# Branch A's product as a stage of its own, with the first head's rotation beside it

## The chip, the cores and the metric

The kernel runs on one core of one Trainium2 chip. The metric is the device time of one execution in microseconds (us); lower is better. The engines named here are TensorE (PE in the profile), VectorE (DVE), ScalarE (ACT), GpSimd (POOL) and SyncE (SP). The last two issue most of the transfers of this kernel and compute almost nothing. ScalarE also issues some stores.

## The reference, cut to what matters

One inference step of a two-layer encoder over 640 tokens: 512 of a prompt and 8 streams of 16. Each layer runs two branches on the same input projection, merges them with gates, projects the result and then runs an MLP.

```python
def _token_mixer(h, shift_prev, s_rwkv, s_ret, pos, p):
    z = h @ p['w_in']
    ...
    y_a, new_rwkv = _rwkv7_branch(za_mix, s_rwkv, p)      # 16 heads of 64, recurrent
    y_b, new_ret = _retention_branch(zb, s_ret, pos)      # 4 heads, key 256, value 512
    merged = (gates[:, :, 0] * (y_a.astype(h.dtype) @ p['w_branch_a'])
              + gates[:, :, 1] * (y_b.astype(h.dtype) @ p['w_branch_b']))
    out = merged.astype(h.dtype) @ p['w_out']

def _retention_branch(zb, s0, pos):
    q, k, v, g = ...
    q, k = rope(q), rope(k) * B_KEY_DIM ** -0.5           # "rotation" below
    # per head: scores, mask with decay, values, old state, new state
    y = y * lax.rsqrt(jnp.mean(y * y, axis=-1, keepdims=True) + NORM_EPS)
    out = jax.nn.silu(g) * y
```

"Branch A's product" is `y_a @ w_branch_a`, a 640 x 1024 by 1024 x 1024 product. The kernel calls it job `ba`.

## The kernel before

Everything lies transposed: channels on the 128 partitions, the 640 tokens along the free axis. A large product is a job of tiles. One tile is 128 output channels, and it is computed as three f32r products per 128 input channels (high x high, low x high, high x low parts), each in two halves of 320 tokens. Job `ba` has 8 tiles of 8 input blocks, so a tile is 48 matmuls. Each of the four jobs `bb0` to `bb3` (a retention head's share of branch B's product) has 8 tiles of 4 input blocks.

**Order within a layer.** Input projection and eight recurrent pairs, then `fz` (the last fill job, beside the group norm of the last pair), then the four retention heads 0 to 3, then `bb3`, the merge, `out`, the MLP. Each engine has its own written-out program, and semaphores join them.

**Units beside a chain.** A head has long chains between engines, so product work is strewn into it. The PE program of a head calls `point("s0")`, `point("y1")` and so on, and each call emits a fixed number of units of a product job (`POINTS`, times `each`). A unit is two input blocks, so 12 matmuls, and a tile of `ba` is four units. Head `h` has `bb{h-1}` beside it; head 0 has `ba`, with `each` = 2. All these units write PSUM banks 0 and 1, so before tile i+1 begins, PE waits (`psum_clear`) until VectorE has taken tile i out. VectorE and ScalarE have programs with the same points:

- VectorE (`sums_of`): at the last unit of a tile it waits for the tile (`mm_done`) and for a gate tile in `ZT`, and writes `ACC[i] = psum * gate` (L2111). At the first unit of the next tile it makes the low part of the weights of two tiles ahead (`split`, L1754, released by ScalarE's high part).
- ScalarE (`high_parts_of`): at the end of each tile it makes the high part of the weights of two tiles ahead (L1274), once they have landed and the tile has been computed.
- SP loads weights into two raw slots. For `ba`, tile i (i of 2 or more), it first waits until tile i-2 has been taken out, then issues the gate load (L504) and the weight load (L505). The last two gate-like tiles made by `fz` are also stored to DRAM by SP (L499), each of them in front of a weight load that comes four tiles later in SP's order. The last of these stores therefore stands behind the loads of `ba`'s tile 2.
- POOL clears `QDP` when the last pair is through, and loads cos and sin, head 0's queries and keys (`QK`), the head's constants, the values (`VY`), and the gate of `ba`'s tile 0 (L607). Then it waits for SP's last store (`z_out`), and only then loads the gate of `ba`'s tile 1 (L607), head 0's swish gate (L594) and the first three blocks of the old retention state (L601).

**A head.** Eight groups of transpositions (values and keys, L677), copied out by ScalarE; then scores, masks and values. Eight steps through the old state (`step`, `st0` to `st7`) go through three buffers `SR`: POOL reads a block (L601), PE multiplies, VectorE updates it (L1743), ScalarE stores it (L1550), and only when the store has landed does POOL read the block three steps on. After the values come square, root, reciprocal and scaling of each token block, the transposition back, the gate, and the split into high and low parts (`lo0` to `lo4`). VectorE rotates the next head's queries and keys in four quarters of six instructions (`rope`), and a last piece of four, in the second half of the head. Head 0's rotation has no head before it. It stands in front of head 0 on VectorE:

```python
                ve.wait_ge(rw_out, 96 * PAIRS * (l + 1))
                for _ in rope(l, 0):
                    pass
                for h in range(RH):
                    retention(l, h)
```

VectorE therefore takes tile 0 of `ba` out only after the whole rotation, and PE's second group of transpositions in a head waits for the rotation.

Of the kernel before, what the change touches and what calls it, by code (L numbers as in the profile page):

```python
# [18 lines left out]
KD = D // 128  # L19
# [212 lines left out]
def build(nc, io, outs, scratch):  # L232
    START, FREED_BY, KT = number_jobs()
# [7 lines left out]
    with ExitStack() as ctx:  # L241
# [44 lines left out]
        AW, _ = cut(at, 2 * 4096)  # L286
# [45 lines left out]
        ZT, _ = cut(SCR - 2 * TOK, 2 * TOK, TOK)  # L332
# [24 lines left out]
        NSR, _ = cut(2 * KD * TOK + 3200, A_COLS)  # L357
        SHR, _ = cut(KD * TOK, A_COLS)
        MS, _ = cut(2 * KD * TOK, KD * TOK, TOK)
        G1, _ = cut(KD * TOK, KD * TOK, TOK)  # L360
# [91 lines left out]
        def units_in(name):  # L452

            n, kt = next((j[1], j[2]) for j in jobs_of_layer() if j[0] == name)
            return n, kt // 2

        def part_of(l, name, emit, each=1):

            tiles_, units = units_in(name)
            at_ = [0]  # L460

            def point(where):
                count = POINTS[where if where in POINTS else where.rstrip("0123456789")] * each
                for _ in range(min(count, tiles_ * units - at_[0])):
                    emit(at_[0] // units, at_[0] % units)
                    at_[0] += 1
            return point

        def beside_head(h):

            return f"bb{h - 1}" if h else "ba"

        def stage_value(stage, n, name):

# [9 lines left out]
        def wait_stage(eng, stage, n, name):  # L484

            eng.wait_ge(stage_sem[stage], stage_value(stage, n, name))
# [177 lines left out]
        def _(pe):  # L664
# [101 lines left out]
                return last  # L766

            def units_of(l, name, each=1):
                g0, units = START[l, name], units_in(name)[1]

                def unit(i, q):

                    g = g0 + i
                    if q == 0:
                        pe.wait_ge(lo_done, g + 1)
                        psum_clear(g)
                    for k in (2 * q, 2 * q + 1):
                        if i == 0 and name == "ba":
                            pe.wait_ge(ya_lo, PAIRS * l + max(4, k + 1))
                        for n_, (w, part) in enumerate(((WH, 0), (WH, 1), (WL, 0))):  # L780
                            for hf in range(2):
                                last = mm(ps[:, hf, 0:HALF], w[:, g % 2, k], operand_of(name, k, part)[:, HALF * hf:HALF * hf + HALF],
                                          start=(k == 0 and n_ == 0), stop=(q == units - 1 and k == 2 * q + 1 and n_ == 2))
                    if q == units - 1:
                        last.then_inc(mm_done, 1)
                return part_of(l, name, unit, each)
# [377 lines left out]
            for l in range(DEPTH):  # L1164

                pe.wait_ge(par_in, 13 * 16 * (l + 1))
                if l:
                    wait_mark(pe, "ve", l - 1, "varf")
                tr(ps[:, 0, 0:106], PR[0:106, 0:128])
                last = tr(ps[:, 0, 106:162], PR[0:56, 128:256])  # L1170
                mark(last, l, "par")
                wait_mark(pe, "ac", l, "silu")
                for k in range(KD):
                    last = tr(ps[:, 2, NSTREAM * k:NSTREAM * k + NSTREAM], CR[0:NSTREAM, 128 * k:128 * k + 128])
                mark(last, l, "ct")
                if l == 0:
                    pe.wait_ge(x_in, 32)
                    wait_mark(pe, "ac", l, "par")
                    wait_mark(pe, "ac", l, "ct")
                    for b in range(NBLK):  # L1180
                        if b == 4:
                            wait_mark(pe, "ac", l, "x0")
                        for k in range(KD):
                            last = tr(ps[:, 2 * (b % 4) + k // 4, 128 * (k % 4):128 * (k % 4) + 128], XR[:, b, 128 * k:128 * k + 128])
                        mark(last, l, f"x{b}")
                    wait_mark(pe, "ac", l, "x4")
                wait_mark(pe, "ac", l, "par")
                wait_mark(pe, "ac", l, "ct")

                for n in range(13):  # L1190
                    m = 12 * l + n
                    if n < 12:
                        pe.wait_ge(ada_in[n % 2], 16 * (6 * l + n // 2 + 1))
                        if n >= 2:
                            pe.wait_ge(ada_row, m - 1)
                        a = AW[:, 4096 * (n % 2):4096 * (n % 2) + 4096].rearrange("p (k n) -> p k n", k=8)
                        for k in range(KD):
                            last = mm(ps[0:NSTREAM, 5 + n % 2, :], CT[:, k], a[:, k], k == 0, k == KD - 1)
                        last.then_inc(ada_used, 1)
                    if n:  # L1200
                        pe.wait_ge(ada_row, m)
                        for j in range(4):
                            t = 4 * (n - 1) + j
                            last = tr(ps[:, 7, NSTREAM * t:NSTREAM * t + NSTREAM], CR[0:NSTREAM, 512 * ((n - 1) % 2) + 128 * j:512 * ((n - 1) % 2) + 128 * j + 128])
                        last.then_inc(ada_turned, 1)
                pe.wait_ge(shr_in, 16 * (l + 1))
                for t in range(A_T):
                    last = tr(ps[:, 2, 8 * t:8 * t + 8], SHR[0:DEC_B, 128 * t:128 * t + 128])
                mark(last, l, "shr")
                wait_mark(pe, "ac", l, "mod")  # L1210
                norm_sums(l, "n0", "sq0", S1)

                gemm(l, "lora", [(l, f"h0.{j}") for j in range(4)])
                gemm(l, "rkv0")
                wait_mark(pe, "ac", l, "lora")
                pe.wait_ge(lw_in, 48 * (l + 1))
                point = units_of(l, "fa")
                for _ in prepare(l, 0):
                    point("pre")
                point("end")  # L1220
                for p in range(PAIRS):
                    rwkv(l, p)
                point = units_of(l, "fz")
                for _ in group_norm(l, PAIRS - 1):
                    point("post")
                point("end")
                wait_stage(pe, "ac_ch", PAIRS * l + PAIRS - 1, "sout")
                for h in range(RH):
                    retention(l, h)
                gemm(l, f"bb{RH - 1}", [(RH * l + RH - 1, "lo4")] * 2)  # L1230
                gemm(l, "out", [(l, f"ms{j}") for j in range(4)])
                psum_clear(START[l, "up0"])
                for t in range(A_T):
                    last = tr(ps[0:NSTREAM, t // 4, 128 * (t % 4):128 * (t % 4) + 128], NSH[:, t])
                mark(last, l, "nsh")
                wait_mark(pe, "ac", l, "nsh")
                norm_sums(l, "mix", "sqm", ACC)
                wait_mark(pe, "ve", l, "varm")
                norm_sums(l, "n1", "sq1", S1)
                for f in range(8):  # L1240
                    gemm(l, f"up{f}", [(l, f"h1.{j}") for j in range(4)] if f == 0 else ())
                    gemm(l, f"down{f}")
                psum_clear(START[l, "down7"] + 8)
                norm_sums(l, "ffn", "sqf", ACC)
# [10 lines left out]
        def _(ac):  # L1255
# [124 lines left out]
                return part_of(l, name, beside)  # L1380

            def high_parts_of(l, name, each):
                g0, units = START[l, name], units_in(name)[1]

                def beside(i, q):

                    if q == units - 1:
                        split_next(g0 + i, (g0 + i) % 2)
                return part_of(l, name, beside, each)
# [258 lines left out]
            for l in range(DEPTH):  # L1648
# [38 lines left out]
                point = evictions_of(l, "fa")  # L1687
# [5 lines left out]
                point = evictions_of(l, "fz")  # L1693
# [4 lines left out]
                for t in range(4, 8):  # L1698
                    wait_stage(ac, "ve_gn", PAIRS * l + t, "ya")
                    do(H[0][:, t], ACC[:, t])  # L1700
                    ac.sem_inc(ya_hi, 1)
                for h in range(RH):
                    retention(l, h)
                gemm(l, f"bb{RH - 1}")
# [27 lines left out]
        def _(ve):  # L1732
# [361 lines left out]

            def sums_of(l, name, each):

                g0, units = START[l, name], units_in(name)[1]

                def beside(i, q):
                    g = g0 + i  # L2100
# [131 lines left out]
            for l in range(DEPTH):  # L2232
# [16 lines left out]
                point = low_parts_of(l, "fa")  # L2249
# [5 lines left out]
                point = low_parts_of(l, "fz")  # L2255
# [7 lines left out]
                    tt(H[1][:, t], ACC[:, t], H[0][:, t].bitcast(F32), SUB)  # L2263
                    ve.sem_inc(ya_lo, 1)
                ve.wait_ge(rw_out, 96 * PAIRS * (l + 1))
                for _ in rope(l, 0):
                    pass
                for h in range(RH):
                    retention(l, h)
# [54 lines left out]
```

## Time and profile before

| | |
|---|---|
| time, median of 3 runs | 4717.69 us (4714.6 to 4718.88) |
| profiled execution | 4717.44 us, span in the trace 4715.7 us |
| PE busy | 91% of the span |
| PE's share of the chain that ended last | 83% |
| VectorE, ScalarE busy | 42%, 30% |
| mean granted TensorE clock | 0.96 of full |

The span is the time from the first to the last instruction in the trace. The engines' busy shares are means over stages with different limits, so the part around the change has to be read by itself: in layer 0 it lies between 1321 us and 1470 us, and in layer 1 between 3655 us and 3802 us.

### The profile page before, as it was taken

The page shows a single profiled execution, that of the slowest core. Times are in us where ns is not written, and L with a number is a line of the kernel's source. Part 1 is how long each engine was busy: PE and PEld are TensorE (multiplying, and loading weights), DVE is VectorE, ACT ScalarE, POOL GpSimd, SP SyncE. Part 2 cuts the span into 40 slices and gives each one's busy share as a digit, 9 for nine tenths or more (in the row PEclk, how much of TensorE's full clock was granted, in tenths as well). Part 3 has the DMA queues.
Part 4 walks back from the last instruction along what each step waited for, and adds up shares of the span by engine and source line. Part 5 has one row for each costly group of instructions (what it writes and reads, how often), then busy time and mean ns, then how long its engine had stood idle before and what let it go on. Part 6 is the DMA issues. An engine that isn't in the chain of part 4 may idle for free.

```text
span 4715.7 us, 85682 instructions
## 1 busy us (share of the span) xinstructions
PE 4286.2 (91%) x37020; PEld 3700.7 (78%) x37020; DVE 1966.9 (42%) x2998; ACT 1397.8 (30%) x2131; POOL 239.9 (5%) x399
## 2 busy tenths in 40 slices
PE   6899999999978887999877999999999788869997
PEld 1688888888965566999816898888888656769996
DVE  0444434444235554444405344444442444444444
ACT  1333333334222222222204333333332222232222
POOL 0000000000011110000000000000000111000000
PEclk9899999999989998999988999999999899989998
DMA  7212212222245542222271212212222554502221
GB/s 243 86 58 63 63 59 63 66 66 63 74 153 196 177 156 63 72 74 72 60 246 42 61 61 63 64 59 63 66 69 72 179 201 162 161 26 76 74 75 59
DMA packets 482303, 448.78 MB, mean 95 GB/s; under 512 B 17894, under 2 KB 399728, under 8 KB 481024
## 3 DMA queue, kind: packets, MB, share of 16 engines
q1 hardware_dynamic: 434352, 294.99, 20.2%
q0 software_dynamic: 30192, 115.10, 7.4%
q10 hardware_dynamic: 17408, 33.56, 1.9%
q8 instruction: 275, 4.51, 0.4%
q14 instruction: 76, 0.62, 0.0%
HBM read 345.82 MB, written 97.76 MB: 94 GB/s over the span
## 4 chain that ended last, share of the span: by engine, by line
PE 83%; DVE 7%; DMA 5%; ACT 3%; issue 2%; POOL 0%; SPq 0%; DVEq 0%; ACTq 0%
PE ps L673 81%; DVE scr L1741 3%; DMA scr<-in_ada_w_dram 2%; PE ps L677 2%; ACT scr L1261 1%; DMA scr<-scratch_z 1%; DMA w_raw<-in_w_branch_a_dram 1%; DVE scr L1743 1%; ACT w_hi L1274 1%; DVE scr L1813 1%; DVE acc L1741 1%; DVE lw L1741 1%; DVE h_lo L1741 0%; DVE w_lo L1754 0%; DMA w_raw<-in_w_in_dram 0%
## 5 line engine op out<-in xcount | busy, mean ns | idle before, releaser
L673 PE MATMUL ps<-h_hi,w_hi 128*128 128x320 f32 x4544 | 1106.4, 325 | 121.1 <-DVEq L1749 76.3
L673 PE MATMUL ps<-scr 64*64 64x64 f32 (+10 forms) x13632 | 986.0, 260 | 67.1 <-DMA scr<-in_ada_w_dram 55.6
L673 PE MATMUL ps<-h_lo,w_hi 128*128 128x320 f32 x4544 | 1044.2, 311 | 0.0
L673 PE MATMUL ps<-h_hi,w_lo 128*128 128x320 f32 x4544 | 1042.2, 311 | 0.0
L673 PEld LDWEIGHTS ps<-scr 64*64 64x64 f32 (+5 forms) x13632 | 624.0, 140 | 384.3 <-issue 349.6
L673 PEld LDWEIGHTS ps<-h_hi,w_hi 128*128 128x128 f32 x4544 | 751.3, 190 | 213.1 <-issue 176.0
L673 PEld LDWEIGHTS ps<-h_lo,w_hi 128*128 128x128 f32 x4544 | 768.9, 190 | 0.0
L673 PEld LDWEIGHTS ps<-h_hi,w_lo 128*128 128x128 f32 x4544 | 767.8, 190 | 0.0
L1274 ACT ACTIVATE w_hi<-w_raw 128x1024 fp32r<-128x1024 f32 (+1 forms) x468 | 410.8, 878 | 820.0 <-PE ps L673 621.3
L1261 ACT ACTIVATE scr<-ps 128x512 f32<-128x512 f32 (+9 forms) x702 | 344.1, 490 | 993.6 <-PE ps L673 754.6
L1754 DVE TENSOR_TENSOR w_lo<-w_raw,w_hi 128x1024 fp32r<-128x1024 f32 (+1 forms) x468 | 469.4, 1003 | 355.0 <-ACT w_hi L1274 334.7
L1741 DVE TENSOR_TENSOR scr<-ps,c 128x512 f32<-128x512 f32 (+2 forms) x416 | 221.2, 532 | 407.0 <-PE ps L673 370.4
L673 PE MATMUL ps<-r_hi,w_hi 128*128 128x320 f32 x1408 | 333.2, 318 | 21.6 <-DVE w_lo L1754 6.5
L673 PE MATMUL ps<-r_lo,w_hi 128*128 128x320 f32 x1408 | 324.1, 312 | 0.0
L673 PE MATMUL ps<-r_hi,w_lo 128*128 128x320 f32 x1408 | 323.5, 311 | 0.0
L677 PE MATMUL ps<-c,scr 128*128 128x128 f32 (+4 forms) x824 | 133.1, 289 | 154.0 <-DMA scr<-scratch_z 38.7
L673 PEld LDWEIGHTS ps<-r_hi,w_hi 128*128 128x128 f32 x1408 | 237.1, 190 | 39.4 <-issue 30.9
L677 PEld LDWEIGHTS ps<-c,scr 128*128 128x128 f32 (+4 forms) x824 | 102.8, 155 | 198.5 <-issue 71.2
L673 PEld LDWEIGHTS ps<-r_lo,w_hi 128*128 128x128 f32 x1408 | 238.7, 190 | 0.0
L673 PEld LDWEIGHTS ps<-r_hi,w_lo 128*128 128x128 f32 x1408 | 238.1, 190 | 0.0
L1378 ACT ACTIVATE scr<-ps 128x640 f32<-128x640 f32 x128 | 90.1, 704 | 379.1 <-PE ps L673 378.4
L1782 DVE TENSOR_TENSOR scr<-ps,scr 128x640 f32<-128x640 f32 (+1 forms) x112 | 92.3, 824 | 202.4 <-PE ps L673 202.4
(143 smaller groups left out, 2969.7 us busy)
## 6 DMA issues: line engine op xcount, KB each, us to landing
w_raw<-in_w_in_dram SPq DMA_DIRECT2D x180, 512.0 KB, 3.7
scr<-in_ada_w_dram SPq DMA_DIRECT2D x24, 2048.0 KB, 7.8
scratch_z<-scr SPq DMA_DIRECT2D x128, 320.0 KB, 2.2
scr<-in_state_ret_dram POOLq DMA_DIRECT2D x64, 512.0 KB, 4.9
out_dram<-scr ACTq DMA_DIRECT2D x64, 512.0 KB, 2.9
w_raw<-in_w_ffn_up_dram SPq DMA_DIRECT2D x64, 512.0 KB, 4.0
w_raw<-in_w_ffn_down_dram SPq DMA_DIRECT2D x128, 256.0 KB, 2.8
scr<-scratch_z POOLq DMA_DIRECT2D x24, 1280.0 KB, 8.1
```

Source lines behind the costliest of these rows:

```text
L673: return pe.matmul(out, lhsT, rhs, start=start, stop=stop, skip_group_check=True)
L677: return pe.transpose(out, in_, c1[0:n, C_ID:C_ID + n])
L1261: ac.activation(out, in_, f, **kw).then_inc(ac_order, 1)
L1274: ac.activation(WH[:, s, 0:kt], WR[:, s, 0:kt], ACT.Copy).then_inc(hi_done, 1)
L1378: ac.activation(halves(ZT[:, f % 2]), two_banks(0), fn).then_inc(psum_read_a, 1)
L1741: tt = lambda o, a, b, op: after(ve.tensor_tensor(o, a, b, op))
L1743: stt = lambda o, a, s, b, o0, o1: after(ve.scalar_tensor_tensor(o, a, s, b, o0, o1))
L1754: ve.tensor_tensor(WL[:, s, 0:kt], WR[:, s, 0:kt], WH[:, s, 0:kt].bitcast(F32), SUB).then_inc(lo_done, 1)
L1782: ve.tensor_tensor(dst, src, dst, ADD).then_inc(psum_read_v, 1)
L1813: after(ve.reciprocal(RS, RS))
```

## The change

Job `ba` is taken out of head 0 and run as a whole before it, on all engines that have a part in it: PE (`units_of(l, "ba")("end")`), ScalarE (`high_parts_of`) and VectorE (`sums_of`). On VectorE the four quarters of head 0's rotation are put behind the first four tiles of `ba`, one behind each; the last piece follows the fifth. Head 0 then has nothing at its points (`beside_head(0)` is None). The programs of SP and POOL are not edited.

```diff
         def part_of(l, name, emit, each=1):
-            tiles_, units = units_in(name)
+            tiles_, units = units_in(name) if name else (0, 0)
...
         def beside_head(h):
-            return f"bb{h - 1}" if h else "ba"
+            return f"bb{h - 1}" if h else None
...
             def units_of(l, name, each=1):
-                g0, units = START[l, name], units_in(name)[1]
+                g0, units = (START[l, name], units_in(name)[1]) if name else (0, 0)
...
                 wait_stage(pe, "ac_ch", PAIRS * l + PAIRS - 1, "sout")
+                units_of(l, "ba")("end")
                 for h in range(RH):
                     retention(l, h)
...
                     do(H[0][:, t], ACC[:, t])
                     ac.sem_inc(ya_hi, 1)
+                high_parts_of(l, "ba", 1)("end")
                 for h in range(RH):
                     retention(l, h)
...
                 ve.wait_ge(rw_out, 96 * PAIRS * (l + 1))
-                for _ in rope(l, 0):
+                turning, point = rope(l, 0), sums_of(l, "ba", 1)
+                for i in range(4 * KD):
+                    point("t")
+                    if i % 4 == 3:
+                        next(turning, None)
+                for _ in turning:
                     pass
                 for h in range(RH):
                     retention(l, h)
```

(`high_parts_of` and `sums_of` get the same guard for a job of None as `units_of`.)

## Rows read from the trace of the kernel before

**Rows 1.** Page, busy time and share of the span.
```profile
PE   4286.2 (91%) x37020; PEld 3700.7 (78%) x37020; DVE 1966.9 (42%) x2998; ACT 1397.8 (30%) x2131; POOL 239.9 (5%) x399
```

**Rows 2.** Windows: start:end and length, busy of PE, PEld, DVE, ACT, POOL, clock, DMA.
```profile
1291.00:1319.00 28.00, 26.11 (x195) 24.78 (x190) 7.15 (x9) 7.58 (x11) 3.60 (x6) 1.00 0.25 84
1321.40:1353.40 32.00, 10.36 (x60) 9.33 (x60) 17.99 (x34) 5.10 (x7) 6.03 (x11) 0.65 0.46 161
1353.40:1457.20 103.80, 94.78 (x536) 70.08 (x536) 45.71 (x69) 25.15 (x47) 13.07 (x21) 0.96 0.55 183
1457.20:1469.30 12.10, 5.32 (x24) 5.05 (x24) 2.42 (x6) 0.63 (x1) 2.16 (x3) 0.80 1.03 389
1469.30:1547.50 78.20, 70.74 (x380) 47.78 (x380) 42.59 (x69) 22.54 (x47) 9.56 (x15) 0.94 0.48 157
...
3686.40:3789.60 103.20, 94.08 (x537) 69.46 (x537) 45.69 (x70) 25.14 (x47) 13.01 (x20) 0.97 0.55 184
```

**Rows 3.** Waits of PE, 1321 to 1470 us: total, times, longest.
```profile
PE ps L677 <- DVEq L1866: 9.8, 1, 9.8
PE ps L677 <- ACTq L1360: 9.5, 3, 6.3
```

**Rows 4.** Timeline of PE: start, duration, instruction, idle before it.
```profile
1301.04 0.54 PE L673 MATMUL ps<-h_hi,w_hi 128*128 128x320 f32 x2 [0.95 <-ACT scr L1378]
...
1321.43 0.53 PE L673 MATMUL ps<-r_hi,w_hi 128*128 128x320 f32 x2 [1.26 <-ACT scr L1378]
...
1328.25 0.46 PE L673 MATMUL ps<-h_hi,w_lo 128*128 128x320 f32 x2
1334.23 1.12 PE L677 MATMUL ps<-c,scr 128*128 128x128 f32 x4 [5.53 <-DMA scr<-scratch_z]
1345.17 1.97 PE L677 MATMUL ps<-c,scr 128*128 128x128 f32 x8 [9.82 <-DVEq L1866]
1353.48 1.11 PE L677 MATMUL ps<-c,scr 128*128 128x128 f32 x4 [6.34 <-ACTq L1360]
```

**Rows 5.** Chain that ended last, around 1354 us: start, length, what.
```profile
1354.60 5.35 PE ps L673 x24
```

**Rows 6.** Timeline of SP's queue.
```profile
1346.57 0.43 SPq L505 DMA_DIRECT2D w_raw<-in_w_branch_a_dram  x1
1347.05 0.58 SPq L499 DMA_DIRECT2D scratch_z<-scr  x1
```

**Rows 7.** Timeline of POOL: the two gate loads.
```profile
1326.40 0.54 POOL L607 DMA_DIRECT2D scr<-scratch_z  x1
1352.91 0.54 POOL L607 DMA_DIRECT2D scr<-scratch_z  x1 [25.97 <-DMA scratch_z<-scr]
```

**Rows 8.** VectorE and ScalarE by form, 1321 to 1457.2 us: count, busy, mean ns.
```profile
L1743 DVE SCALAR_TENSOR_TENSOR scr<-scr,ps 128x1024 f32<-128x1024 f32 x8 | 9.7, 1216 | 1.3 <-PE ps L673 1.2
L1754 DVE TENSOR_TENSOR w_lo<-w_raw,w_hi 128x1024 fp32r<-128x1024 f32 x7 | 8.6, 1225 | 15.4 <-ACT w_hi L1274 15.0
...
L1741 DVE TENSOR_TENSOR scr<-scr 128x320 f32<-128x320 f32 x16 | 7.9, 492 | 0.5
L2111 DVE TENSOR_TENSOR acc<-ps,scr 128x640 f32<-128x640 f32 x8 | 6.6, 824 | 14.1 <-PE ps L673 13.3 <-DVE lw L2153 0.6 <-DVE lw L1741 0.2
```
```profile
L1274 ACT ACTIVATE w_hi<-w_raw 128x1024 fp32r<-128x1024 f32 x7 | 7.4, 1057 | 76.8 <-DMA w_raw<-in_w_branch_a_dram 76.8
...
L1261 ACT ACTIVATE scr<-ps 128x512 f32<-128x512 f32 x11 | 6.5, 591 | 6.8 <-PE ps L673 5.9 <-ACT scr L1261 0.5
```

**Rows 9.** DMA issues of the execution: count, KB each, median us to landing.
```profile
scr<-in_state_ret_dram POOLq DMA_DIRECT2D x64, 512.0 KB, 4.9
out_dram<-scr ACTq DMA_DIRECT2D x64, 512.0 KB, 2.9
...
scr<-scratch_z POOLq DMA_DIRECT2D x24, 1280.0 KB, 8.1
...
w_raw<-in_w_branch_a_dram SPq DMA_DIRECT2D x16, 512.0 KB, 4.3
```

More of the change, by code:

```diff
@@ L1382, in high_parts_of @@
             def high_parts_of(l, name, each):
-                g0, units = START[l, name], units_in(name)[1]
+                g0, units = (START[l, name], units_in(name)[1]) if name else (0, 0)
                 def beside(i, q):
@@ L2095, in sums_of @@
             def sums_of(l, name, each):
-                g0, units = START[l, name], units_in(name)[1]
+                g0, units = (START[l, name], units_in(name)[1]) if name else (0, 0)
                 def beside(i, q):
```

## The prediction

> **What bounds the kernel now.** I read the page first: TensorE is busy 91% of the span [rows 1]. So a change pays where TensorE waits, and costs where it uncovers a wait. Then the windows around the change [rows 2]. From the first matmul of `ba` (1321.4) to 1353.4 us TensorE works 10.4 of 32.0 us, at 0.65 of its clock: that is the hole before head 0. In the rest of head 0 (1353.4 to 1457.2) it works 94.8 of 103.8 us, at 0.96. Layer 1 has the same head (94.1 of 103.2), so I work out one layer and double it.
>
> The waits and the timeline of PE say what the hole is made of [rows 3, 4]. Tile 0 of `ba` runs from 1321.4 to 1328.5. TensorE then waits 5.5 us for the values of head 0, 9.8 us for the rotation on VectorE and 6.3 us for ScalarE. The last is no slow copy: ScalarE is in order and stands at the high part of tile 2's weights, whose load SP issued only at 1346.6 [rows 6], because VectorE took tile 0 out only after the rotation. The three waits are 21.7 us, and the change aims at them. The whole stretch that it touches runs from 1321.4 to head 1's first transposition at 1469.3, which is 147.9 us.
>
> **Part 1: the product as a stage.** A tile takes 7.1 us at full clock, from 1321.43 to the last pair at 1328.25 plus its 0.3 us [rows 4], a unit 1.76 us, eight tiles 56.8 us. All tiles use the same two banks and nothing lies between them now, so each hand-over is bare.
>
> - *Tile 0 to 1.* VectorE must have the gate of tile 0, which POOL issues at 1326.4 behind the values of head 0 [rows 7]. These free TensorE at 1334.2 [rows 4]; the gate should follow at about 1335. With 0.82 us of eviction [rows 8] tile 1 starts at 1336.0: wait 7.5 us.
> - *Tile 1 to 2.* The queues that were not edited decide. SP's last store comes right behind the weight load of tile 2, and POOL loads the gate of tile 1 only when it has landed: before, 1347.05 to 1352.91, 5.9 us [rows 6, 7]. Now tile 0 is out at 1335.9, SP's store issues at 1336.8, the gate load at 1342.7, and it lands about 4.5 us later (my choice, by the 4.3 us of a weight load [rows 9]). Tile 2 starts at 1348.2; tile 1 ended at 1344.9: wait 3.3 us.
> - *Tile 2 to 3.* POOL now sends the swish gate and three state blocks (2.8 MB) while tile 3's weights load. 4.3 us [rows 9] becomes about 8 (estimate: the stretch at 389 GB/s was full [rows 2]): wait 4.0 us.
> - *The other four.* SP can load tile i+2 only when tile i is out, then comes 0.45 us of issue, 4.3 us of load [rows 9], 1.06 us of ScalarE and 1.23 us of VectorE [rows 8]: 7.1 us, as long as the tile in between. Then the 0.82 us of eviction. Four gaps of 1.15 us: 4.6 us.
> - *Clock.* After a wait of some microseconds 24 matmuls took 5.35 us [rows 5] where two units take 3.5. Three restarts at 1.8 us: 5.4 us.
>
> Stage: 56.8 + 7.5 + 3.3 + 4.0 + 4.6 + 5.4 = 81.6 us. The rotation costs nothing here: a quarter is six instructions of 0.49 us, some 3.1 us [rows 8], in the 5 to 6 us in which VectorE would wait for weights. Without that cover it would be 12.6 us.
>
> **Part 2: head 0 bare.** Its own time bounds it from below: 103.8 us less the 28 units in it (49.3 us) is 54.5, plus 1.3 for the two groups of transpositions before it at full clock: 55.8 us. Head 1 gives nearly the same with its own units: 78.2 less 14 x 1.76 is 53.6 us [rows 2]. This supposes that the units covered nothing. What they covered, each estimated from rows:
>
> - ScalarE's copies of the transpositions, 0.59 us each against 0.44 us of four transpositions: about 1.4 us.
> - Old state: three buffers, and a block comes back only after update (1.2 us), store (2.9) and read (4.9), with issues some 10 us [rows 8, 9]. TensorE's own work between two uses of a buffer is about 8 us. Steps 3 and 4: 3.0 us together.
> - Square, root, reciprocal and scaling of the first block before it can be turned back: 1.8 us. One more restart at half clock: 1.0 us.
> - Second half: VectorE has gates, updates, low parts and four rotation quarters of the next head in one queue, about 20.5 us between the first gate and the last update, where TensorE has some 10 us of its own. Most of that stands in the 55.8 already: 2.0 us more.
>
> Sum 9.2, so 65.0 us. Behind the VectorE instructions queued there wait the steps, hence the stores and POOL's next reads.
>
> **Part 3: into head 1.** Between head 0 and head 1's transpositions lay 12.1 us at 389 GB/s [rows 2]: the product `m` (2.5 MB) was being stored as head 1's values were read. Now `m` can go out once POOL has issued head 0's last state read, over 15 us sooner, and the read takes its usual 8.1 us [rows 9]: a gain of 4.0 us.
>
> **Sum.** 81.6 + 65.0 + 8.1 = 154.7 us against 147.9: 6.8 us longer per layer, 13.6 in all. The change takes away most of the 21.7 us, but pays 4.6 + 7.3 us of new hand-overs in the stage and uncovers 9.2 us in the head. From the profiled execution (4717.4, span 4715.7, median of the runs 4717.7, so the same) that is 4731 us.
>
> Two levels of clock are seen: 1.2 GHz after waits, 2.4 GHz otherwise. In `fz`, where each tile ends in a gap of 0.95 us before ScalarE's copy [rows 4], the granted clock stayed at 1.00 [rows 2], so I charge the four short gaps nothing. The Trainium skill, TensorE: Matmul & The Clock Gate, "A second HAM failure mode: psum-queue depth-cycling", speaks against this change: small idle times between groups of matmuls that take turns on PSUM can make the clock swing. By that rule the four short gaps would each cost a restart of 1.8 us too, 7.2 us per layer, and the time would be 4745 us. The trace agrees for waits over some 2 us, not for gaps of 1 us.
>
> **Rivals.**
>
> - *The head shrinks to its own work.* The state reads land as TensorE asks, and the quiet queues shorten parts 1 and 2: 78 + 55.8 + 8.1 = 141.9, 6.0 us less per layer, 4705 us. To be faster by 0.2% a layer must come to 143.2 us, so the bare head to 53.5 us with my stage of 81.6, or to 57.1 with a stage of 78. For it: head 1 in its own window comes to 53.6. Against it: three buffers and a 10 us round trip. 9%.
> - *It cancels.* The head uncovers 3 to 6 us instead of 9, or the weight load of tile 3 isn't slowed: 147 to 152 us per layer, 4716 to 4726 us. 28%.
> - *The clock stays down in the bare head.* There the waits come close together, as at 1353 us, where 24 matmuls ran at half clock [rows 5]. TensorE's own 45 us would be half at 1.2 GHz: some 10 us more, a third of it hidden. 13.6 + 14 gives 4745 us. 10%, with the four gaps of the stage going the same way.
> - *The change doesn't hide the rotation*, because VectorE's first quarter waits for queries and cos, and with it the low part of tile 2's weights. These came at 1331 us before, in time for tile 0's eviction, so nothing: under 2%, in the second case.
>
> **How the numbers follow.** My forecast, 4727 to 4741, has 53%. A measurement of this kernel tells 0.2% from no change, 9.4 us, so the bounds are 4708 and 4727. Faster is the first rival: 9%. Same is the second: 28%. Slower is the forecast and the clock: 63%. The terms that are estimates (7.3 us of waits at tiles 1 to 3, 9.2 us in the head) can each be half or one and a half, twice over the layers: 16 us either way, together with both outer rivals 4705 to 4755.
>
> **What would show it.** In the profile after: PE busy with `w_branch_a`'s units alone for about 80 us from 1321, with gaps of about 7, 3, 4 and four of 1.1 us; the second gate load of POOL (L607) near 1343 instead of 1353; no wait of PE on the rotation; head 0's transpositions near 1403; waits of PE on state reads in head 0, which were none before; head 1's transpositions near 1476 instead of 1469. I would be wrong if head 0 took under 58 us, if the gaps between tiles 1 and 3 were missing, or if PE's clock fell in the whole head.

## The result and the profile after

| | median us | runs | lowest to highest |
|---|---|---|---|
| before | 4717.69 | 7 | 4710.47 to 4723.00 |
| changed | 4732.01 | 7 | 4728.96 to 4740.81 |

The ratio is 1.0035 [1.0023, 1.0046]: slower by 14.3 us, where 13.6 was forecast (4731 us). The profiled execution of the changed kernel took 4733.55 us with a span of 4731.8; before it was 4717.44 and 4715.7. The mean granted clock is 0.962 in both.

The page says nothing by itself: TensorE has 12 us more of busy time and the same share as in [rows 1].

```profile
PE   4298.1 (91%) x37020; PEld 3709.5 (78%) x37020; DVE 1967.4 (42%) x2998; ACT 1398.1 (30%) x2131; POOL 239.7 (5%) x399
```

The windows of the changed kernel answer to [rows 2] (same columns). The first three are layer 0: the stage of `ba`, head 0 bare, and the way into head 1. The next three are the same in layer 1, then head 1 of layer 0.

```profile
1320.20:1405.00 84.80, 63.79 (x386) 62.15 (x387) 30.24 (x47) 10.51 (x12) 8.88 (x15) 0.88 0.49 159
1405.00:1469.70 64.70, 50.09 (x213) 21.47 (x210) 33.27 (x56) 20.23 (x42) 10.17 (x16) 0.87 0.55 190
1469.70:1477.30 7.60, 5.32 (x25) 5.06 (x25) 2.42 (x6) 0.63 (x1) 2.15 (x3) 0.78 1.00 387
3664.30:3747.40 83.10, 62.09 (x386) 60.46 (x387) 30.23 (x47) 10.58 (x12) 8.95 (x15) 0.90 0.50 162
3747.40:3809.10 61.70, 47.87 (x213) 20.68 (x211) 33.27 (x56) 20.24 (x42) 10.18 (x16) 0.92 0.60 212
3809.10:3816.30 7.20, 3.84 (x25) 3.58 (x25) 2.42 (x6) 0.63 (x1) 2.15 (x3) 0.91 0.90 321
1477.30:1555.50 78.20, 70.82 (x396) 47.76 (x397) 44.19 (x74) 22.52 (x47) 11.69 (x18) 0.98 0.52 170
```

Layer 0 takes 84.8 + 64.7 + 7.6 = 157.1 us, against 147.9 before. Layer 1 takes 83.1 + 61.7 + 7.2 = 152.0; before it was 146.4 (from 3655.3 to 3801.7 in its timeline). That is 9.2 and 5.6 us longer, 14.8 of the 16.1 us between the two spans. A second profiled execution of the same kernel (E5) gives 6.3 and 8.9 us, 15.2 in all: the sum holds, its split between the layers does not. The last row shows that head 1 is what it was [rows 2], 78.2 us, so the loss lies in the stretch that the change touches.

The waits of PE from 1320 to 1480 us answer to [rows 3] (total, times, longest):

```profile
PE ps L673 <- DVE acc L2113: 21.0, 7, 8.1
PE ps L673 <- DMA scr<-in_state_ret_dram: 7.0, 3, 4.5
PE ps L673 <- DVEq L1868: 3.1, 2, 2.3
PE ps L677 <- ACTq L1361: 2.7, 3, 1.9
PE ps L677 <- DMA scr<-scratch_z: 2.3, 1, 2.3
```

The rotation and ScalarE's 6.3 us are gone, as the change meant it. In their place stand seven hand-overs of the stage at 21.0 us (the three waits that it removes came to 21.7), and 7.0 us of waits on state reads that were not there before. The timeline of PE, which answers to [rows 4], shows the seven (one of 1.01 us left out), then the first waits of the bare head and head 1's transposition:

```profile
1335.52 0.87 PE L673 MATMUL ps<-r_hi,w_hi 128*128 128x320 f32 x2 [8.06 <-DVE acc L2113]
1345.98 0.53 PE L673 MATMUL ps<-r_hi,w_hi 128*128 128x320 f32 x2 [1.01 <-DVE acc L2113]
1360.00 0.87 PE L673 MATMUL ps<-r_hi,w_hi 128*128 128x320 f32 x2 [6.74 <-DVE acc L2113]
1370.20 0.53 PE L673 MATMUL ps<-r_hi,w_hi 128*128 128x320 f32 x2 [1.01 <-DVE acc L2113]
...
1387.92 0.69 PE L673 MATMUL ps<-r_hi,w_hi 128*128 128x320 f32 x2 [2.17 <-DVE acc L2113]
1397.74 0.53 PE L673 MATMUL ps<-r_hi,w_hi 128*128 128x320 f32 x2 [1.01 <-DVE acc L2113]
...
1427.15 1.70 PE L673 MATMUL ps<-scr,lw 128*32 128x256 f32 x12 [2.22 <-DMA scr<-in_state_ret_dram]
...
1449.16 3.09 PE L673 MATMUL ps<-scr,lw 128*32 128x256 f32 x12 [4.48 <-DMA scr<-in_state_ret_dram]
1469.71 0.63 PE L673 MATMUL ps<-h_hi,w_hi 128*128 128x320 f32 x2 [2.26 <-DVEq L1868]
1477.29 2.04 PE L677 MATMUL ps<-c,scr 128*128 128x128 f32 x16 [2.27 <-DMA scr<-scratch_z]
```

Read the pair's duration beside the wait ahead of it: 0.53 us at 2.4 GHz, 0.87 us at 1.2. It tells the clock at the start of a tile only; whether the clock stayed is told by the tile's whole length. The chain of work that ended last (it answers to [rows 5]) shows what each hand-over hangs on, and how long the 48 matmuls of a tile take after it:

```profile
1325.15 9.27 DMA scr<-scratch_z
...
1335.52 9.47 PE ps L673 x48
...
1346.27 10.44 DMA w_raw<-in_w_branch_a_dram
1356.74 1.06 ACT w_hi L1275
1357.96 1.08 issue
1359.04 0.83 DVE acc L2113
1360.00 9.20 PE ps L673 x48
...
1370.20 7.28 PE ps L673 x48
...
1418.11 4.17 DMA out_dram<-scr
1422.57 4.44 DMA scr<-in_state_ret_dram
...
1440.94 2.83 DMA out_dram<-scr
1444.05 4.97 DMA scr<-in_state_ret_dram
```

Tile 1 starts when the gate of tile 0 has landed: 9.27 us from its issue. Tile 3 starts when its weights have landed: 10.44 us, where the median of this load is 4.4. In head 0 the chain goes twice from a store of old state (`out_dram`) to the read of the next block into the same buffer. The first read ends at step 4 of the eight (1427.15), the second at step 7 (1449.16). POOL's queue answers to [rows 7]:

```profile
1325.15 0.54 POOL L607 DMA_DIRECT2D scr<-scratch_z  x1
1341.52 0.54 POOL L607 DMA_DIRECT2D scr<-scratch_z  x1 [15.83 <-DMA scratch_z<-scr]
...
1444.76 0.57 POOL L622 DMA_DIRECT2D scratch_m<-acc  x1
```

### The profile page after: what moved, and what is told of

Its sections match the earlier page's. It is cut to its first block, busy times and chain, and to the rows that moved or that the text cites. A ratio compares the mean times of both kernels' runs of the same rounds, so it can differ in the third digit from the quotient of the medians.

```text
span 4731.8 us, 85692 instructions
## 1 busy us (share of the span) xinstructions
PE 4298.1 (91%) x37020; PEld 3709.5 (78%) x37020; DVE 1967.4 (42%) x2998; ACT 1398.1 (30%) x2131; POOL 239.7 (5%) x399
## 4 chain that ended last, share of the span: by engine, by line
PE 83%; DVE 7%; DMA 6%; ACT 3%; issue 2%; POOL 0%; SPq 0%; DVEq 0%; ACTq 0%
PE ps L673 80%; DMA scr<-in_ada_w_dram 2%; DVE scr L1743 2%; PE ps L677 2%; DMA scr<-scratch_z 1%; ACT scr L1262 1%; DVE scr L1745 1%; DVE scr L1815 1%; DMA w_raw<-in_w_branch_a_dram 1%; ACT w_hi L1275 1%; DVE acc L1743 1%; DVE h_lo L1743 1%; DMA w_raw<-in_w_in_dram 0%; DVE w_lo L1756 0%; DMA out_dram<-scr 0%
```

## The experiments

Each ratio is to the kernel before in the same job, with its 95% interval. Before's median was 4719.8 us in the first job (E1 to E4), 4720.8 in the second (E5 to E8) and 4717.8 in the third (E9 to E12). So a run is set beside the changed kernel by what each lies over before in its own job; the changed kernel is 14.3 us over it, and 15.0 in E5. Lengths of stretches are those of each run's one profiled execution. Line numbers after the edits shift by up to seven.

**E1. Is the rotation hidden by the stage?** On VectorE, whole head first, tiles behind:

```diff
-                turning, point = rope(l, 0), sums_of(l, "ba", 1)
-                for i in range(4 * KD):
-                    point("t")
-                    if i % 4 == 3:
-                        next(turning, None)
-                for _ in turning:
+                for _ in rope(l, 0):
                     pass
+                sums_of(l, "ba", 1)("end")
```

> The product stays a stage of its own, but the first head's rotation stands whole in front of it on VectorE, as before the change. My theory (the stage has room for the rotation, and tile 0's eviction is what the next tile waits for): tile 1 starts about 9.5 us later in each layer, the rest keeps its form: 4751 us, 4746 to 4756. Rival (the rotation's quarters delay VectorE's weight parts and evictions, and that makes the gaps of the stage): 4732 us or less, with gaps of tiles 2 to 7 shorter than in the changed kernel.

4747.07 us, 1.0055 [1.0042, 1.0069]: 27 us over before, so some 13 us over the changed kernel. Tile 1 waits for the whole rotation:

```profile
1347.52 0.87 PE L673 MATMUL ps<-r_hi,w_hi 128*128 128x320 f32 x2 [18.49 <-DVE acc L2113]
```

So the rotation in front costs 6 to 7 us per layer by the medians; in the profiled execution the stage is 92.7 and 93.1 us long, 8 and 10 us more. In the changed kernel the stage's waits for weights and gates do hide it.

**E2. Is the burst in front of tile 3's weights the cause of its wait?** SP's last store of `fz` frees POOL's queue; here it goes ahead of tile 2's loads:

```diff
+                        if name == "ba" and i == 2:
+                            store(g - 3)
```

> The changed kernel, with SyncE's last store of fz put in front of the loads of ba's tile 2, so that GpSimd's gate of tile 1, swish gate and first state blocks go out before the stage's second half. My theory (that chain makes the 6.7 and 7.1 us waits of tile 3): these go to about 1 us with their restart at half clock, 7 us per layer, 4718 us, 4714 to 4723. Rival (the weight loads are slow in a stage without cover whatever runs beside them): the waits of tile 3 stay, 4730 us or more.

4728.63 us, 1.0020 [1.0011, 1.0029]: 8.9 us over before, so a gain of 5 to 6 us where I expected 14. The stage is 79.8 and 80.9 us long, 4.9 and 2.1 us shorter. Tile 3's wait is gone and tile 2's has grown:

```profile
1337.54 0.87 PE L678 MATMUL ps<-r_hi,w_hi 128*128 128x320 f32 x2 [7.95 <-DVE acc L2118]
1350.34 0.87 PE L678 MATMUL ps<-r_hi,w_hi 128*128 128x320 f32 x2 [3.37 <-DVE acc L2118]
1361.16 0.53 PE L678 MATMUL ps<-r_hi,w_hi 128*128 128x320 f32 x2 [1.01 <-DVE acc L2118]
```

The burst now meets the weights of tile 2, which need 9.21 us in this kernel's chain:

```profile
1337.85 9.21 DMA w_raw<-in_w_branch_a_dram
```

**E3. Half a stage.** Four tiles in front with the rotation's quarters, the other 16 units beside head 0, in all three engines' orders:

```diff
-                units_of(l, "ba")("end")
+                beside0 = units_of(l, "ba", 1)
+                beside0(16)
                 for h in range(RH):
-                    retention(l, h)
+                    retention(l, h, beside0)
```

> Four tiles of ba as a stage in front of head 0 (a quarter of the rotation behind each), the other four as units beside head 0, one per point as in heads 1 to 3. My theory (the hole of 22 us is worth filling with three to four tiles, and a head needs the rest as cover): per layer about 49 us of stage, 84 us of head, 10 us into head 1: 143 us, 4708 us in all, 4700 to 4714. Rival (what makes the changed kernel slower is the stage itself, its gaps and waits at tiles 1 to 3, not the bare head): 4725 us or more, since those tiles are all still in front.

4721.99 us, 1.0003 [0.9994, 1.0012]: between my 4708 and the rival's 4725 or more. It is 2.2 us over before, which wins back some 12 us of the changed kernel's loss, and not in the hole, where tiles 1 and 3 still wait 6.88 and 6.42 us, but where head 0 has its units beside it. In its stead the way into head 1 waits 7.6 us (2.3 in the changed kernel).

**E4. Does the order of ScalarE's queue hold back head 0's last state block?** ScalarE's `store(4)` goes ahead of its `root(3, 17)` in head 0.

> The changed kernel, with ScalarE's store of head 0's state block 4 put in front of the root of token block 3 (block 7 is read when it has landed). My theory (in the second half of the bare head VectorE's queue ends just behind the state reads; in layer 1 TensorE waited 4.0 us for VectorE at this step already): the wait of 4.5 us on a state block in layer 0 turns into a wait on VectorE, at most 1 us gained per layer: 4731 us, 4728 to 4734. Rival (the state's round trip sets the length of the bare head): 4 us per layer less, 4724 us.

4733.52 us, 1.0025 [1.0016, 1.0034]: 13.7 us over before, no gain clear of the noise. The wait of 4.48 us on the state read became 1.59 us on VectorE in layer 0, and in layer 1 it is still 3.92, on VectorE:

```profile
3789.11 3.09 PE L673 MATMUL ps<-scr,lw 128*32 128x256 f32 x12 [3.92 <-DVEq L1871]
```

The shorter wait in layer 0 can't be put down to the edit: E5, without it, waits 2.29 us there.

**E5. The changed kernel again**, with no edit, as a yardstick for the second job.

> The changed kernel once more, unedited, beside the others of this job on the same chip. Both theories: the ratio to the kernel before is 1.0035 again (1.002 to 1.0045); the two layers together are about 15 us longer from the first matmul of ba to head 1's first transposition.

4735.89 us, 1.0031 [1.0021, 1.0042]. Its bare heads take 63.4 and 64.6 us.

**E6. The state's round trip.** Old state isn't stored in head 0:

```diff
+                    if h == 0:
+                        ac.sem_inc(sr_out[i % 3], 16)
+                        return
                     ac.dma_start(outs[7]
```

> The changed kernel without ScalarE's eight stores of the old retention state in head 0 (left out in both layers, so that state isn't returned for that head); GpSimd's reads go on as soon as VectorE has updated the block. My theory (state round trips cost 3 to 4 us of the bare head, and behind them the queue of VectorE waits): PE's waits on state reads in head 0 go to nothing, a wait on VectorE stays, 3 us per layer less than the changed kernel: 4726 us. Rival (the round trip is what sets the bare head's length): 7 us or more per layer less, 4718 us or lower.

4726.41 us, 1.0013 [1.0004, 1.0022]: 9.5 us under E5, 4.7 per layer. The bare heads take 59.9 and 60.0 us, and no wait on a state read is left in them. The five reads of a head took no less time (4.8 and 4.9 us at the median in the two layers, 4.2 and 4.2 in E5), so it is the earlier issue that helps, and not that 4 MB less are moved beside them. What was behind it is VectorE, at step 7, 3.92 us in both layers (layer 0 shown):

```profile
1442.71 3.09 PE L673 MATMUL ps<-scr,lw 128*32 128x256 f32 x12 [3.92 <-DVEq L1871]
```

**E7. VectorE's queue.** The quarters of head 1's rotation are left out of head 0:

```diff
-                turning = rope(l, h + 1) if h < RH - 1 else iter(())
+                turning = rope(l, h + 1, h > 0) if h < RH - 1 else iter(())
```

> The changed kernel without the rotation of head 1's queries and keys inside head 0 (left out in both layers; 12.6 us of VectorE), the last piece of the rotation stays in its place. My theory (in the second half of the bare head VectorE's queue is the longest, and the state reads are just before it): 3 to 5 us per layer less, 4724 us, and the state reads are then what the last step waits for. Rival (VectorE isn't what the bare head waits for; the state round trip is): under 1 us per layer, 4731 us.

4733.84 us, 1.0023 [1.0014, 1.0032]: 2 us under E5, within the noise, as the rival said; I had expected 4724. The bare heads of its profiled execution are no shorter, 64.4 and 68.3 us. Step 7 waits for the state read now, 4.04 us in layer 0 (shown) and 4.83 in layer 1:

```profile
1443.95 2.65 PE L673 MATMUL ps<-scr,lw 128*32 128x256 f32 x12 [4.04 <-DMA scr<-in_state_ret_dram]
```

E4, E6 and E7 together: step 7 of the bare head has two things that come late, the read and VectorE's queue, within about 1 us of each other. Whichever is taken away, the other keeps the step at 3.9 to 4.8 us. E6 gains all the same, because it clears the earlier steps too (in E5 these waited 3.4 us for reads in layer 0).

**E8. Three tiles in front**, as E3 with `beside0(12)` and 16 units at the points of head 0, one at each; four are left for its end.

> Three tiles of ba as a stage in front of head 0, 16 units beside head 0 at one per point, and the last four units at the end of head 0, where TensorE otherwise waits for the last low part and for head 1's values. My theory (a tile in front beyond the first two or three costs its 8.3 us in full, a unit in a hole costs nothing): about 7 us per layer less than four tiles in front, 4709 us, 4704 to 4716, faster than before. Rival (units at the end of the head are no better placed than in the stage, since m is stored later and head 1's first eviction waits for it): 4720 us, as with four tiles.

4736.85 us, 1.0031 [1.0020, 1.0042]: against 4709 expected and 4720 by the rival, both missed. The rival had named the late store of `m`, but not its price. POOL's queue shows it:

```profile
1458.18 0.58 POOL L622 DMA_DIRECT2D scratch_m<-acc  x1 [31.23 <-DVE acc L2115]
...
1460.03 0.76 POOL L594 DMA_DIRECT2D scr<-scratch_z  x1
...
1461.33 0.75 POOL L590 DMA_DIRECT2D scr<-scratch_z  x1
```

Since `ba` ends only at the head's end, the store of `m` waits 31 us for its last eviction, and behind it in the queue stand a state block, the swish gate (L594) and head 1's values (L590). The values themselves are not held up, they are issued as TensorE ends its last unit. But now everything goes out within some 5 us, 7.0 MB, and moves at 354 GB/s (share 0.98). So the values land late; first the chain, then the timeline of PE:

```profile
1461.33 17.55 DMA scr<-scratch_z
```
```profile
1478.92 3.68 PE L677 MATMUL ps<-c,scr 128*128 128x128 f32 x16 [17.15 <-DMA scr<-scratch_z]
```

Layer 1 waits 17.5 us there. In the changed kernel these waits are 2.3 and 3.4 us.

**E9. Both gates ahead of head 0's data.** E2, and in POOL's order the loop over the two gate loads moved up right behind the `memset` of `QDP`.

> The changed kernel, with SyncE's last store of fz early (as in e2) and GpSimd loading the two gate tiles of ba before head 0's data instead of behind it. My theory (the waits of tiles 1 to 3, 7 to 8, 1 to 3 and 6 to 7 us, come from the order of the queues, and one burst of head 0's data, 5.5 MB, has to pass weights somewhere): tile 1 starts 1 us after tile 0, one wait of some 6 us is left at tile 2, 9 us per layer less than the changed kernel, 4718 us, 4712 to 4724. Rival (those waits only move to another tile): 4728 us or more.

4734.00 us, 1.0034 [1.0023, 1.0045]: the rival was right, the wait only moved. Tile 1 waits 1.07 us instead of 8.06, and tile 2:

```profile
1350.46 0.87 PE L678 MATMUL ps<-r_hi,w_hi 128*128 128x320 f32 x2 [14.36 <-DVE acc L2118]
```

The chain says why. Tile 2's weights are issued early, at 1329, but beside head 0's data:

```profile
1329.14 18.04 DMA w_raw<-in_w_branch_a_dram
```

**E10 to E12. Shorter stages with these queues**: three, two and four tiles in front, the rest beside head 0 (E10 with two units at each `y` point, E11 with two at each `s`, `y` and `x` point, so that `ba` ends before the head's end; E12 with one).

> The queues as in e9; three tiles of ba in front of head 0, twenty units beside it (two at each of the points y0 to y3, one at the others), none at its end, so that m is stored and head 1's values are read as early as before. My theory (cover for the whole head, stage only as long as the hole): per layer some 33 us of stage, 91 us of head, 10 us into head 1, 134 us against 148: 4700 us, 4692 to 4708. Rival (the units are worth the same in either place): 4718 us, as e9.

> As e10 with two tiles in front and 24 units beside head 0 (two at each point s, y and x). My theory: the rotation of head 0 ends some 5 us after tile 1, so the hole isn't quite filled: 4702 us, 4694 to 4712, near e10.

> As e10 with four tiles in front and 16 units beside head 0, one at each point (e3 with the new order of the queues). My theory: e3 less 9 us per layer, 4704 us, 4698 to 4712. Rival (e3's stage was not held by the queues): 4720 us.

| tiles in front | median us | ratio |
|---|---|---|
| E10, three | 4719.14 | 1.0002 [0.9993, 1.0011] |
| E11, two | 4715.61 | 0.9997 [0.9988, 1.0006] |
| E12, four | 4719.42 | 1.0002 [0.9993, 1.0011] |

All miss my 4700 to 4704 and are level with before: not even E11's 2 us are clear of the noise. In each, one tile waits 14.4 to 15.7 us for weights beside the burst, in both layers; E10 and E11 then wait 3.0 and 4.8 us for the rotation as well. These rows are E11's:

```profile
1350.08 0.87 PE L678 MATMUL ps<-r_hi,w_hi 128*128 128x320 f32 x2 [15.11 <-DVE acc L2120]
1360.43 1.97 PE L682 MATMUL ps<-c,scr 128*128 128x128 f32 x8 [4.79 <-DVEq L1875]
```

**The hole is ended by data.** The same 24 us (1321 to 1345) in four kernels, in this order: E1, which is the changed kernel with the rotation in front, the changed kernel, E2, E9.

```profile
1321.00:1345.00 24.00, 7.28 (x48) 7.04 (x48) 16.39 (x30) 4.30 (x6) 5.72 (x10) 0.72 0.45 165
```
```profile
1321.00:1345.00 24.00, 15.91 (x93) 15.42 (x91) 9.26 (x13) 3.78 (x5) 8.08 (x14) 0.79 0.70 239
```
```profile
1321.00:1345.00 24.00, 14.79 (x85) 14.54 (x85) 8.95 (x13) 4.83 (x7) 9.13 (x15) 0.79 0.92 337
```
```profile
1321.00:1345.00 24.00, 14.03 (x95) 13.53 (x93) 8.22 (x12) 3.02 (x5) 8.38 (x14) 0.91 0.94 333
```

Once tile 0 is taken out early (which frees SP's queue) and the loads stand further forward, more of the same bytes move in these 24 us (4.0, 5.7, 8.1 and 8.0 MB). The load of tile 2's weights beside them takes longer: 4.6 us in the changed kernel, 9.2 in E2, 18.0 in E9. The waits of tiles 1 to 3 come to 15.8 us in the changed kernel, 12.3 in E2 and 16.4 in E9. Most of what a queue gives one tile it takes from the next.

## Why the prediction held

**The stage: 81.6 forecast, 84.8 and 83.1 measured.** By its own terms:

| term | forecast | layer 0 | layer 1 |
|---|---|---|---|
| eight tiles | 56.8 | 58.2 (8 x 7.28) | 58.2 |
| tile 0 to 1 | 7.5 | 8.1 | 6.9 |
| tile 1 to 2 | 3.3 | 1.0 | 2.3 |
| tile 2 to 3 | 4.0 | 6.7 | 7.1 |
| the other four | 4.6 | 5.2 | 4.7 |
| restarts | 5.4 | 5.6 | 3.9 |

A tile takes 7.28 us, not 7.1: I had counted the last pair as 0.3 us, and it takes 0.46. Two of the waits were mis-sized, in opposite directions. At *tile 1 to 2* the gate load was issued as forecast (both 21.3 us after the stage's first matmul), but it took 3.1 us in layer 1 (3685.4 to 3688.6) where I had chosen 4.5, and tile 1 ended later than forecast, 24.8 us after the first matmul in layer 0 and not 23.5, since it started later and took 9.47 us, restart included, for 8.9. At *tile 2 to 3* I took the load beside the swish gate and the state blocks as 8 us; it took 10.44, and tile 2, which had no restart, covered 7.3 us of it and not 8.9. E2 shows that this term is real and is the burst's. The restarts came at tiles 1, 3 and 6 in layer 0 and at tiles 1 and 3 in layer 1, not at 1, 2 and 3. The last four gaps are shorter than 1.15 us where the loads keep up (1.01, which is the eviction of 0.83 us and its hand-over) and 2.2 us where one took 5.9 us.

**The bare head: 65.0 forecast, 64.7 and 61.7 measured**, 63.4 and 64.6 in E5. That the head is not 55.8 us without its units was the step that decided the sign, and E6 shows its largest part by removal: 4.7 us per layer hang on the round trip of old state, forecast at 3.0 with the rest in VectorE's queue and the copies. The sum was nearer than its parts, and in that it was lucky. The 55.8 us hold 9.0 us in which TensorE stood [rows 2] and so 46.8 of work. Bare, it stood for 14.6 and 13.8 us and worked 50.1 and 47.9: waits grew by 5.6 and 4.8 us where the terms gave 8.2, and the work, at a lower granted clock, by 3.3 and 1.1 us where the restart had 1.0. The waits also came elsewhere: none at step 3, 2.2 and 1.1 us at step 4, and 4.5 and 4.0 us at step 7, which I had under the 2.0 us of VectorE's queue. There both end together (E6, E7). The other terms of the 9.2 (copies 1.4, first block 1.8) were tried by no run of their own.

**Into head 1: 8.1 forecast, 7.6 and 7.2 measured.** The store of `m` was issued at 1444.8, 25 us before head 1's values, which then took their 7.3 us. The stretch is 4.5 and 4.9 us shorter than before. E8 shows its reverse: where `m` goes out with the values, TensorE waits 17 us.

**The rivals.** The head did not shrink: of the 81.6 + 53.5 us that a gain needed, the stage alone took 1.5 to 3.2 more and the head 8 to 11 more. The clock did not stay down in the head: 0.87 and 0.92 granted over it, with TensorE busy for 50.1 and 47.9 us where its own work is 45 to 47, so 1 to 5 us more and not 10. (At 1353 us before, the half clock held for some two thirds of the 24 matmuls, not for all.) The rotation cost nothing: TensorE has no wait on it, and E1 gives the price of having it in front. The outer bound of 4755 us follows from no term: the terms reach 4747, the rival of the clock 4745.

**The clock and the short gaps.** After a gap of 1.01 us the next pair took 0.53 us and the tile 7.28 (2.4 GHz), four times in layer 0; after 6.7 and 8.1 us the pair took 0.87 (1.2 GHz) and the tile 9.2 to 9.5. Between them it isn't settled by the length alone. In layer 0 a gap of 2.17 us gave a tile of 8.8 us, in the changed kernel and in E5, while 2.10 us in E9, 2.80 in E5's layer 1 and 3.13 in E8 left it at 7.27. So the forecast's line at "some 2 us" isn't a sharp one. And a pair of 0.53 us doesn't prove a fast tile: in E5 it opened one of 8.8. The Trainium skill, TensorE: Matmul & The Clock Gate, "A second HAM failure mode: psum-queue depth-cycling", had been weighed as a rival of 4745 us, a restart at each short gap. For gaps of 1 us the trace doesn't agree with that rule: none of them cost a restart, in layer 0 or in layer 1.

**Where the expected gain went.** The three waits removed were 21.7 us per layer. The stage's seven hand-overs cost 21.0 us, its restarts 4 to 6 us, and the uncovered head some 6 to 9 us over its own 55.8; 4.5 to 4.9 us come back before head 1. E3 and E11 show the other side: with 16 or 24 units beside head 0 again the time is that of before, though single tiles in the hole still wait 6 to 15 us.

No version was faster than the kernel before by its interval. That the rest of the hole is the transfer of head 0's data fits the four windows and the load times. A run with less data there was not made, so how small the hole would be without it stays open.

## What to carry to other kernels

Taking work from beside a chain and putting it into a stage of its own pays only if both halves stand alone: the stage needs its inputs a tile ahead, and the chain needs no cover, which has to be read off its round trips through DRAM and its in-order queues. When several waits stand behind one another in a hole, removing one shows the next: price the hole by the bytes that must arrive in it. And before a loop is moved, look for what waits for its last item in a shared queue, what stands behind that, and what will then be moved at the same time.

## What the runs showed of the hardware

- One weight load of 512 KB took 4.4 us at the median, 9.2 and 10.4 us beside about half of head 0's data (E2, changed) and 18.0 us beside nearly all of it (E9). The whole moved 333 to 337 GB/s over 24 us at a DMA share of 0.92 to 0.94, and 387 over the 7.6 us before head 1. Issuing the load earlier into this full stretch didn't bring it earlier: counted from the stage's first matmul, E9 issued tile 2's at 8.7 us and had it at 26.7, E2 at 15.5 and 24.8.
- In E8 a wait of 31 us in POOL's in-order queue, ahead of the store of `m`, gathered 7.0 MB into one stretch. A 1280 KB load in it took 17.55 us, against 7.30 in the changed kernel, and TensorE waited 17.2 and 17.5 us.
- Step 7's wait was 3.92 us on VectorE to the hundredth in both layers of E6 and in layer 1 of E4. Where a transfer ends it, the same program gave 4.48 us in one execution and 2.29 in another (changed and E5, layer 0).
